# Dilated attention of a two-layer block: values times probabilities for two query tiles in one group of matmuls

## The reference, cut to what matters

```
q, k, v = jnp.split(u @ w_in, 3, axis=-1)
q = apply_partial_rope(split_heads(q, A_HEADS_2), cos, sin)
k = apply_partial_rope(split_heads(k, A_HEADS_2), cos, sin)
v = split_heads(v, A_HEADS_2)
for window, dil in A_PATTERNS:
    ...
    o, lse = banded_attention(by_residue(q)[..., None, :, :], by_residue(k), by_residue(v),
                              radius, A_BLOCK)
    ...
w = jax.nn.softmax(jnp.stack(lses), axis=0)
o = jnp.einsum('pbhs,pbhsd->bhsd', w, jnp.stack(outs))
return merge_heads(o).astype(u.dtype) @ w_out
```

## Time and profile before

| | us |
|---|---|
| three runs: lowest, median, highest | 3055.53, 3055.98, 3058.98 |
| span of the profiled execution, from first to last instruction | 3057.7 |
| the attention loop in it, first scores to the last copy's start | 1428.74 to 1545.27 |
| TensorE matmuls busy, whole span | 2869.8 (94%) |
| TensorE's mean granted clock, whole span | 0.981 |

### The profile page before, as it was taken

The page is one execution under the profiler, slowest core; times in us unless marked ns, Lnnn a source line. Parts: engine busy times, 40 slices in busy tenths (PEclk is TensorE's granted clock), DMA queues, the critical chain, the costliest instruction groups (busy, mean ns, idle before and its releaser), DMA issues.

```text
span 3057.7 us, 32673 instructions
## 1 busy us (share of the span) xinstructions
PE 2869.8 (94%) x12660; PEld 1923.4 (63%) x12660; DVE 1136.5 (37%) x2314; ACT 669.1 (22%) x1520; POOL 517.5 (17%) x789
## 2 busy tenths in 40 slices
PE   8999998789999988899999999999998899999998
PEld 4565543244655432387657588888685566688887
DVE  4543311135343111324623243354436732333354
ACT  3332210023222100102622211100204522211100
POOL 3101111121011111112310012200213610012201
PEclk9999999999999999899999999999999999999999
DMA  3104599941135999622012122222221021122122
GB/s 148 69 29 186 205 420 412 403 152 49 49 135 202 387 417 407 235 83 83 1 58 80 54 76 92 83 76 82 77 100 38 1 83 55 58 104 87 69 76 90
DMA packets 121908, 421.38 MB, mean 138 GB/s; under 512 B 9232, under 2 KB 13456, under 8 KB 95504
## 3 DMA queue, kind: packets, MB, share of 16 engines
q1 hardware_dynamic: 108528, 383.62, 32.9%
q0 software_dynamic: 12640, 33.45, 2.9%
q10 hardware_dynamic: 576, 2.10, 0.2%
HBM read 408.64 MB, written 27.26 MB: 143 GB/s over the span
## 4 chain that ended last, share of the span: by engine, by line
PE 76%; DMA 11%; issue 5%; DVE 3%; ACT 2%; POOL 2%; POOLq 1%; DVEq 0%; SPq 0%; ACTq 0%
PE ps L2371 33%; PE ps L406 10%; DMA ring_feat<-in_w 9%; PE ps L2604 5%; PE ps L1079 4%; PE ps L1603 4%; PE ps L2577 3%; PE ps L1643 2%; PE ps L2478 2%; PE ps L2624 2%; PE ps L2934 2%; PE ps L1866 1%; PE ps L1855 1%; PE ps L1878 1%; DMA tmp<-normed,route_i 1%
## 5 line engine op out<-in xcount | busy, mean ns | idle before, releaser
L406 PE MATMUL ps<-ring_feat 128*96 128x512 f32 (+3 forms) x768 | 305.5, 554 | 5.7 <-DMA ring_feat<-in_w_lat 3.0
L2371 PE MATMUL ps<-ring_feat 128*128 128x256 f32 x1216 | 276.9, 379 | 0.8 <-ACT big L282 0.8
L2371 PE MATMUL ps<-big 128*128 128x256 f32 x1200 | 268.1, 379 | 0.0
L2371 PEld LDWEIGHTS ps<-ring_feat 128*128 128x128 f32 x1216 | 231.0, 190 | 33.4 <-issue 2.1
L2371 PEld LDWEIGHTS ps<-big 128*128 128x128 f32 x1200 | 228.0, 190 | 31.0
L406 PEld LDWEIGHTS ps<-ring_feat 128*128 128x128 f32 (+1 forms) x768 | 139.3, 184 | 155.4 <-issue 118.0
L1603 PE MATMUL ps<-big,tmp 128*64 128x512 f32 x512 | 121.7, 624 | 31.9 <-DMA big<-in_w 27.7
L1603 PE MATMUL ps<-ring_feat,tmp 128*64 128x512 f32 x512 | 124.0, 633 | 27.4 <-DMA ring_feat<-in_w 24.2
L2604 PE MATMUL ps<-ring_feat 128*128 128x512 f32 x320 | 139.4, 592 | 0.7 <-ACT ring_feat L1960 0.7
L1618 DVE TENSOR_TENSOR tmp<-tmp,ps 128x256 f32<-128x256 f32 x32 | 13.5, 421 | 323.6 <-ACT tmp L1612 323.6
L2371 PE MATMUL ps<-tmp 128*128 128x256 f32 x576 | 128.2, 379 | 0.0
(11 more groups left out here) (478 smaller groups left out, 4698.8 us busy)
## 6 DMA issues: line engine op xcount, KB each, us to landing
big<-in_w SPq DMA_DIRECT2D x48, 2048.0 KB, 17.7
ring_feat<-in_w SPq DMA_DIRECT2D x48, 2048.0 KB, 15.9
ring_feat<-in_w_gate_up SPq DMA_DIRECT2D x22, 2048.0 KB, 8.1
ring_feat<-in_w_mix_in SPq DMA_DIRECT2D x12, 2048.0 KB, 8.2
ring_feat<-in_w_down SPq DMA_DIRECT2D x12, 1536.0 KB, 6.8
tmp<-in_w_mem_kv SPq DMA_DIRECT2D x6, 2048.0 KB, 20.7
ring_feat<-in_w_out SPq DMA_DIRECT2D x4, 2048.0 KB, 8.9
big<-expert_out SPq DMA_DIRECT2D x16, 512.0 KB, 7.9
```

The lines of the kernel that those rows point to most:

```text
L406: yield T.matmul(bank, lhs(k), rhs(k), start=k == 0, stop=k == n - 1)
L2371: m = T.matmul(to, lhs[:, j, :], rhs[:, j, :], start=start and j == 0, stop=stop and j == chunks - 1)
```

## The change

`output` is called at even i only, for the pair of units i-4 and i-3. It has the same eight matmuls in the program, each with a moving operand of 256 queries in place of 128. `l_probT` becomes two buffers of two units each (the same memory), and a copy writes its unit's half of it. The count of `l_out` goes up once for a pair, so its waits count pairs, up to `PAIRED` = 16 in place of 32; the waits on it in the later layer are shifted by the same number.

```diff
-        l_probT = [view(tmp, 6144 + i * 1024, 2, TT, P) for i in range(4)]
+        l_probT = [view(tmp, 6144 + i * 2048, 2, TT, 2 * P) for i in range(2)]
...
+        PAIRED = UNITS // 2
+
+        def l_probT_of(n):
+            return l_probT[n // 2 % 2][:, :, :, n % 2 * P:(n % 2 + 1) * P]
...
-            def output(n):
-                c, t = divmod(n, TT)
-                pe.wait_ge(l_probT_act, n + 1)
-                pe.wait_ge(l_probT_dve, n + 1)
-                if t == 0 and c:
+            def output(b):
+                c, half = divmod(b, 2)
+                pe.wait_ge(l_probT_act, 2 * b + 2)
+                pe.wait_ge(l_probT_dve, 2 * b + 2)
+                if half == 0 and c:
                     pe.wait_ge(l_out_read, c)
                 for s in range(TT):
                     for j in range(2):
                         at = 2 * D + c * P + j * HD
-                        m = T.matmul(ps[j * HD:(j + 1) * HD, 6, t * P:(t + 1) * P], qkv[:, s, at:at + HD],
-                                     l_probT[n % 4][:, j, s, :], start=s == 0, stop=s == TT - 1)
+                        m = T.matmul(ps[j * HD:(j + 1) * HD, 6, half * 2 * P:(half + 1) * 2 * P], qkv[:, s, at:at + HD],
+                                     l_probT[b % 2][:, j, s, :], start=s == 0, stop=s == TT - 1)
                 m.then_inc(l_out, 1)
...
-                if 0 <= i - 3 < UNITS:
-                    output(i - 3)
+                if 0 <= i - 3 < UNITS and i % 2 == 0:
+                    output((i - 4) // 2)
...
                 if n >= 4:
-                    dve.wait_ge(l_out, n - 3)
-                V.tensor_copy(l_probT[n % 4][:, 1], ps[:, 5, :].rearrange("p (s q) -> p s q", s=TT)).then_inc(l_probT_dve, 1)
+                    dve.wait_ge(l_out, n // 2 - 1)
+                V.tensor_copy(l_probT_of(n)[:, 1], ps[:, 5, :].rearrange("p (s q) -> p s q", s=TT)).then_inc(l_probT_dve, 1)
...
             def finish(c):
-                act.wait_ge(l_out, (c + 1) * TT)
+                act.wait_ge(l_out, (c + 1) * TT // 2)
```

More of the change, by code:

```diff
@@ L1954, in copy_probs @@
                 if n >= 4:
-                    act.wait_ge(l_out, n - 3)
-                A.activation(l_probT[n % 4][:, 0], ps[:, 4, :].rearrange("p (s q) -> p s q", s=TT), ACT.Copy).then_inc(l_probT_act, 1)
+                    act.wait_ge(l_out, n // 2 - 1)
+                A.activation(l_probT_of(n)[:, 0], ps[:, 4, :].rearrange("p (s q) -> p s q", s=TT), ACT.Copy).then_inc(l_probT_act, 1)
             def finish(c):
-                act.wait_ge(l_out, (c + 1) * TT)
+                act.wait_ge(l_out, (c + 1) * TT // 2)
                 A.activation(featv[:, c, :], ps[:, 6, :], ACT.Copy).then_inc(l_out_read, 1)
@@ L2120, in finish @@
                 c, t = divmod(n, TT)
-                dve.wait_ge(l_out, U0 + n + 1)
+                dve.wait_ge(l_out, PAIRED + n + 1)
                 V.tensor_copy(qkv[:, t, c * P:(c + 1) * P], ps[:, 5 + n % 2, 0:P]).then_inc(d_read, 1)
@@ L2181, in copy_diff @@
                 if n >= 3:
-                    act.wait_ge(l_out, U0 + n - 2)
+                    act.wait_ge(l_out, PAIRED + n - 2)
                 A.activation(d_probT[n % 3], ps[:, 4, :].rearrange("p (s q) -> p s q", s=TT), ACT.Copy).then_inc(d_probT_ready, 1)
@@ L3369, in run @@
                     dilated(name, eng, l)
-                    qkv_free[0] = (l_out, UNITS)
+                    qkv_free[0] = (l_out, PAIRED)
                 else:
```

## The result

The changed kernel takes **3073.0 us** (median of 5 runs, 3072.16 to 3074.78) against 3058.83 us for the kernel before, run beside it (5 runs, 3055.53 to 3060.07). The ratio is **1.0049, with a 95% interval of 1.0038 to 1.0061**: slower by 14 to 15 us. Forecast was 3069.6 us, 13.6 us more than the 3055.98 known then. The profiled span grew from 3057.7 to 3072.7 us. Of these 15.0 us, 0.77 lie ahead of the loop (its first scores start at 1429.51, not 1428.74), 0.56 behind it, and 13.67 in it. The total is known less well than the loop: the median of the kernel before ran from 3055.90 to 3058.83 us over the four comparisons of this document.

The account below looks back on a forecast made before the run. Two-iteration chains from odd scores over VectorE and ScalarE to the next odd scores bound the attention loop. Six periods 10.2, two more hops 1.7, pair 0.85 and end 0.83 gave +13.6 on 3055.98: 3069.6 us, range 3062 to 3076.

Parts of the forecast that it names:

- the odd iterations' saving is lost: Output groups removed from odd iterations, 1.02 us each: time given back becomes TensorE idling ahead of turn_probs in even iterations.
- The hops set the pace: Attention loop: two-iteration chains from odd scores through VectorE and ScalarE to next odd scores; 6.64 becomes 7.49, 7.56 becomes 8.41.
- The wide group: Output group on TensorE with 256 columns: 1.94 us against 1.09, so the group behind starts 0.85 later.
- The link doesn't shrink: Odd scores to turn_probs, over table, exponentials and copy: stays 4.62 us, or 5.10 with queries, when TensorE runs ahead.
- ScalarE's copy, not GpSimd or issue, ends the wait: Even iterations: turn_probs waits 0.45 and 0.50 us for ScalarE's copy of unit i-3 to free banks 4 and 5.
- The sum: Loop from scores(3) to last copy to featv: 10.2 + 1.7 + 0.85 + 0.83 = +13.6 us.
- the uncovered copy at the end: Loop's end: last pair waits for VectorE's copy; last copy to featv 3.93 us after last turn_probs, +0.83.
- TensorE's work as the pace: Rival, attention loop: only TensorE's work counts, −2.7 us, 3053.3; chance 0.07, and 0.03 with the waits gone, 3046.6.
- Half of it absorbed: Rival: ScalarE or VectorE starts earlier as TensorE runs ahead, a pair costs half, +6.8, 3062.8 us; chance 0.03.
- No overlap at 256 columns: Rival: two heads' halves of the array stream one by one in output, 27 us on top, 3096.8; chance 0.02.
- The clock stayed at 1.00: Against the rival that TensorE's clock falls once in each of seven periods, 14 us more, 3083.6; chance 0.05.
- a change of tiling mode drains TensorE: Skill rule cited for output groups: every group removed saves one drain; speaks for the change, whose TensorE work sum is −2.7 us.

Follow-up runs that it names:

- e8_even_only: Changed kernel with the first unit of each pair left out, one narrow output group in even iterations only; loop −0.12 us against before, ratio 1.0004.
- e2_two_narrow: Kernel before with two 128-wide output groups (units i-4, i-3) at each even i, none at odd i; loop +13.09 us, ratio 1.0043.
- e5_pair_filled: Changed kernel with the wide group of units i-6, i-5 between scores and turn_probs at even i; loop −4.25 us against before, ratio 0.9989.

## Why the prediction was right

Its steps can be read off the traces, and the experiments show the one that was only argued, that the odd iterations' saving is lost.

*The hops set the pace.* Predicted 7.49, 8.41, period 15.90; measured 7.49, 8.42, 15.91. That the saving of the odd iterations counts for nothing was argued from one trace; e8_even_only shows it.

*The wide group.* Predicted 1.94 us, from sixteen instructions at 128 and at 512 columns; measured 1.95, and the group behind it starts 0.85 later, as predicted. The two heads' halves overlap at 256 columns as well.

*The link doesn't shrink.* It is 4.62 and 5.11 us in the changed kernel, and was 4.62 and 5.10.

*ScalarE's copy, not GpSimd or issue, ends the wait.* Read from 0.07 us between copy and load; shown by the swap on ScalarE in both kernels.

*The sum.* Predicted: six periods +10.2, two more hops +1.70, the pair behind turn_probs +0.85, the uncovered copy at the end +0.83. Measured from scores(3) on: 1559.71 − 1437.73 = 121.98 against 1545.27 − 1436.92 = 108.35, +13.63. The terms, from the two traces: six periods +10.23, two more hops and the pair behind turn_probs together +2.55, the end +0.85. (The first of the six periods is longer than the others in both kernels, 16.03 us in one, 1437.73 to 1453.76, and 14.33 in the other, so it adds 1.70 as they do.) The time behind the loop grew by 0.56, ahead of it by 0.77, where the kernels run the same code; the first scores of the traces here scatter by four microseconds, so nothing speaks for an effect of the change. The median came out 3.4 us above the forecast, of which 2.85 is the median of before having been 3058.83 in this comparison, and not 3055.98. So that the loop's +13.6 came out to a few hundredths is the mechanism; that the medians of this comparison differ by 14.2, so close to it, is in part luck, since the median of before moved by 3 us from one comparison to the next.

*The rivals.* TensorE's work as the pace: −2.7 forecast, refuted here; TensorE's work sets the pace only in the kernels whose waits were removed. Half of it absorbed: the link did not move by more than 0.01 us. No overlap at 256 columns: the group takes 1.95 us, not over 3. The clock stayed at 1.00 with TensorE busy 85.94 of 105 us, in gaps of up to 1.46 us, and behind them through one of 2.47 at the loop's end. Against this stands the stretch ahead of the loop in the kernel before, where TensorE idled for 1.72, 0.69 and 0.85 us, one after the other with 0.6 to 0.7 us of work between, and the granted clock then fell to 0.50. No single idle stretch there was as long as the 2.47 us, so the agreement that the prediction saw there with a rule on long idle stretches is weaker than it says; what separates the two cases no run here shows. The prediction cited the Trainium skill, TensorEngine Tiling, section Key Properties, by which a change of tiling mode drains TensorE, and each removed group saves one. The weight loads in the traces are idle for 0.17 us where turn_probs is followed by a group of 64 columns or 64 rows. A saving of that size is there: two narrow groups without a change of shape between them take 1.89 us in e2_two_narrow, where two apart take 2.05. What the array does in that time no row shows. Here the saving fell into the odd iterations and was lost.

## What to carry to other kernels

In a software-pipelined loop with lags of two iterations find the hop that closes the loop over the other engines, and ask in which iterations its TensorE part lies: batching work into every second iteration lengthened each second hop here by the full extra and shortened hops that did not matter. Before making work on the busiest engine cheaper, look for waits ahead of a buffer's reuse and for the queue in which the freeing copy stands; two steps swapped on ScalarE were worth more (6.4 us) than the pairs could be (2.7 by the sum of the work). A wait put down to an engine that was done half a microsecond earlier, or to "issue", is worth a look at what ended just before it: here the true releaser ended 0.05 us (GpSimd), 0.07 (ScalarE) and 0.12 (VectorE, in e5_pair_filled, from 1474.89 to the weight load at 1475.01) ahead.

## What had not been expected of the hardware

In the output groups the fixed time goes with the change of shape more than with the number of instructions: sixteen more narrow ones behind the first sixteen add 0.86 to 0.87 us, not 1.02, as much as doubling the width does (0.85). What also stands out is how exactly the loop repeats: hops agree to 0.01 us between kernels that differ only off the hop (7.56 and 6.64 in the kernel before and in the one with half of its outputs gone), while everything ahead of the loop scatters by some 4 us from trace to trace (first scores at 1425.3 to 1429.5). A change of a few microseconds in such a loop is read better from its own stretch of the trace than from the total.
